# The rotation of a recurrence by columns instead of by pairs of heads

## What is computed

```python
w_log = -softplus(-(w0 + tanh(wd) @ w2)) - 0.5
decay = exp(-exp(w_log))
a = sigmoid(a0 + ad @ a2)
kk = k * k_k;  kk = kk / max(norm(kk), 1e-12)          # per head of 64
k = k * (1.0 + (a - 1.0) * k_a)
# 8 heads; the scan runs over 1024 tokens, computed in chunks of 64
state, y = scan(rwkv7_step, state0, (r, decay, k, v, -kk, kk * a))
y = groupnorm(y) * lnx_g + lnx_b
bonus = sum(r * k * r_k, axis=-1) * v
y = y + bonus
# beside it: attention of 8 heads over a band of 576 keys, on other columns of the same projection
x = x + gate * (concat([y_r * silu(g_r), y_a * silu(g_a)]) @ w_out)
```

## Time and profile before

| | us |
|---|---|
| median of 3 runs (2422.2 to 2427.26) | 2424.62 |
| the profiled execution's own time | 2418.48 |
| its span in the trace | 2416.6 |
| mean granted TensorE clock of it, share of full speed | 0.972 |

### The profile page before, as it was taken

The page is one execution under the profiler, slowest core; times in us unless marked ns, Lnnn a source line. Parts: engine busy times, 40 slices in busy tenths (PEclk is TensorE's granted clock), DMA queues, the critical chain, the costliest instruction groups (busy, mean ns, idle before and its releaser), DMA issues. The chain is left out here.

```text
span 2416.6 us, 43216 instructions
## 1 busy us (share of the span) xinstructions
PE 2277.8 (94%) x18830; PEld 1848.8 (77%) x18830; DVE 1456.7 (60%) x2456; ACT 937.6 (39%) x1532; POOL 78.7 (3%) x61
## 2 busy tenths in 40 slices
PE   7999988999999999999999999999999998789789
PEld 5777767788888888888878888778777776567667
DVE  5575866565434886777753454646455655767743
ACT  4446432444333443333342433354333232335441
POOL 0000000000000000000000000002000001200000
PEclk9999989999999999999999999989999999799989
DMA  5332252544123232222365534333323113111044
GB/s 179 88 94 66 69 170 71 173 123 129 53 62 119 77 96 83 79 79 86 93 196 164 157 90 135 98 113 110 109 80 107 51 37 97 41 44 44 3 129 150
DMA packets 329349, 238.15 MB, mean 99 GB/s; under 512 B 10948, under 2 KB 288580, under 8 KB 329032
## 3 DMA queue, kind: packets, MB, share of 16 engines
q1 hardware_dynamic: 326424, 229.82, 31.7%
q10 hardware_dynamic: 2736, 5.57, 0.6%
HBM read 202.33 MB, written 33.03 MB: 97 GB/s over the span
## 5 line engine op out<-in xcount | busy, mean ns | idle before, releaser
L1525 PE MATMUL PS<-SR 128*128 128x512 f32 (+2 forms) x1696 | 681.6, 402 | 43.2 <-DVE SR L2106 34.8
L1526 PE MATMUL PS<-SR 128*128 128x512 f32 (+2 forms) x1696 | 659.9, 389 | 0.0
L1527 PE MATMUL PS<-SR 128*128 128x512 f32 (+2 forms) x1696 | 659.7, 389 | 0.0
L2106 DVE TENSOR_TENSOR SR<-SB,SR 128x1024 fp32r<-128x1024 f32 (+1 forms) x240 | 289.1, 1206 | 289.8 <-ACT SR L2967 289.5
L1525 PEld LDWEIGHTS PS<-SR 128*128 128x128 f32 (+1 forms) x1696 | 320.4, 189 | 128.3 <-DVE SR L2106 36.9
L1527 PEld LDWEIGHTS PS<-SR 128*128 128x128 f32 (+1 forms) x1696 | 320.2, 189 | 68.7
L1526 PEld LDWEIGHTS PS<-SR 128*128 128x128 f32 (+1 forms) x1696 | 320.9, 189 | 62.2 <-issue 1.7
L2967 ACT ACTIVATE SR<-SB 128x1024 fp32r<-128x1024 f32 (+1 forms) x240 | 247.5, 1033 | 254.9 <-DMA SB<-in_w_down 116.1
L1546 PE MATMUL PS<-SR 128*128 128x512 f32 x624 | 243.4, 390 | 0.3 <-DVE SR L2232 0.3
L1548 PE MATMUL PS<-SR 128*128 128x512 f32 x624 | 242.8, 389 | 0.0
L1547 PE MATMUL PS<-SR 128*128 128x512 f32 x624 | 242.7, 389 | 0.0
(11 more groups left out here) (315 smaller groups left out, 3032.2 us busy)
## 6 DMA issues: line engine op xcount, KB each, us to landing
SB<-in_w_in SPq DMA_DIRECT2D x110, 512.0 KB, 4.0
SB<-in_w_up SPq DMA_DIRECT2D x88, 256.0 KB, 3.3
SB<-in_w_out SPq DMA_DIRECT2D x32, 512.0 KB, 4.2
SB<-in_w_down SPq DMA_DIRECT2D x32, 512.0 KB, 4.1
SB<-in_w_ada SPq DMA_DIRECT2D x12, 1024.0 KB, 5.2
hidden<-SB SPq DMA_DIRECT2D x22, 512.0 KB, 3.4
SB<-hidden SPq DMA_DIRECT2D x43, 256.0 KB, 5.3
asides<-SB SPq DMA_DIRECT2D x36, 256.0 KB, 4.1
```

The costliest lines, as they stand in the source:

```text
L1525: pe.matmul(out, whi[:, k - k0, :], hi[k], start=(k == 0), stop=False)
L1526: pe.matmul(out, whi[:, k - k0, :], lo[k], start=False, stop=False)
L1527: i = pe.matmul(out, wlo[:, k - k0, :], hi[k], start=False, stop=(k == j.K - 1))
L2106: v.tensor_tensor(m.f32r(a, kn * cn), m.f32(a, kn * cn), m.f32r(a + 1024, kn * cn).bitcast(F32), SUB).then_inc(*on("split.v", p))
```

## The change

A turn of the rotation now takes one recurrence step's 128 columns of all four tiles (`prep_a(half, c)`, `c` 0 to 3) instead of one tile's 512 columns. `pres` starts step `cp` as soon as its own turn (`("rot", cp)`) has been written, and turns 1 1 to 1 3 stand between recurrence steps 4 and 5. The key norm `kn` and the scratch A, B, C, D get places of their own in memory (one set in place of up to three), taken from 4096 words per partition that the build had reserved and the kernel did not use (`dynamic_dma_scratch_size=SCRATCH`, `TOTAL` larger by 4304); the table of ones and zeros for the scan moves to another place and is loaded earlier (`load_resets`). 1 + (a - 1) k_a is made by four ACT instructions on 128 columns each; the scan is four scans of 128 columns; the bonus's factor r_k goes into the small matrix that PE multiplies by (`rkbo`). The bonus is copied out once per turn.

```diff
-        self.kn, self.rot = part(26624, work(8192, 2048)), part(28672, work(10240, 2048))
+        self.kn = [tiles(v3(work(32816, 2048), 4)) for _ in range(2)]
+        self.rot = [work(34864 + 512 * i, 512) for i in range(4)]
...
     def prepare(self, half, places):
-        yield from self.room((places, 1))
-        b, free = places.take()
-        ahead = half
-        for j in range(4 + ahead):
-            if j < 4:
-                yield from self.after(("lora", half, j), *["v1"] * (half and j % 2))
-                yield [("prep_a", half, j)]
-            if j >= ahead:
-                yield [("prep_m", half, j - ahead, b, free), ("prep_b", half, j - ahead)]
-        places.give(b, ("prep.v", "bon", half))
-        yield [("prep_bon", half, b)]
+        yield from self.after(("lora", half, 3))
+        for c in range(4):
+            if half and c > 1:
+                yield from self.after(("read", 2 + c))
+            yield [("prep_a", half, c)]
+            yield from self.room((places, 1))
+            b, free = places.take()
+            places.give(b, ("prep.v", "bon", half, c))
+            yield [("prep_m", half, c, b, free), ("prep_b", half, c), ("prep_bon", half, c, b)]
+            self.done.add(("rot", 4 * half + c))
...
     def pres(self):
-        yield from self.after("prep0", "gemm0")
+        yield from self.after("gemm0")
         for cp in range(8):
-            if cp > 1:
-                yield from self.after(("seq", cp - 2))
-            if cp == 4:
-                yield from self.after("prep1", "g1")
+            yield from self.after(("rot", cp), f"g{cp // 4}", f"v{cp // 4}", *[("seq", cp - 2)] * (cp > 1))
             yield from self.pre(cp)
...
     def prepared(cp):
-        half = cp // 4
-        w.wait_ge(*at("prep.v", "9", half, 3))
-        w.wait_ge(*at("prep.g", "c", half, 3))
+        w.wait_ge(*at("prep.v", "9", cp // 4, cp % 4))
+        w.wait_ge(*at("prep.g", "c", cp // 4, cp % 4))
...
+    def prep_a(half, c):
+        A, B, C, D = m.rot
+        sl = slice(128 * c, 128 * c + 128)
+        w.wait_ge(*at("prep.a", "1", half, c))
+        w.wait_ge(*at("hs.v", "o", f"kk{half}", 3))
+        v.tensor_tensor(m.kk4[:, :, sl], h4(A), m.kk4[:, :, sl], MUL).then_inc(*on("prep.v", "1", half, c))
         w.wait_ge(*at("rs64", 0))
+        w.wait_ge(*at("lora.a", "s", half, 0, 3))
+        for e in turn_before(half, c):
+            w.wait_ge(*e)
+        for j in range(4):
+            i = v.tensor_tensor_scan(B[:, 128 * j:128 * j + 128], m.rs64[:, 0:128], m.sg[half][j][:, sl], 0.0, MUL, ADD)
+        i.then_inc(*on("prep.v", "4", half, c))
+        w.wait_ge(*at("prep.v", "4", half, c))
+        v.tensor_tensor(h4(A), h4(B), m.sg4[half][:, :, sl], SUB).then_inc(*on("prep.v", "5", half, c))
+        w.wait_ge(*at("shift.v", "o", f"r{half}", 3))
+        v.tensor_tensor(h4(D), m.rr4[half][:, :, sl], m.kk4[:, :, sl], MUL).then_inc(*on("prep.v", "3", half, c))
...
+    def prep_a(half, c):
+        A, B, C, D = m.rot
+        w.wait_ge(*at("lora.a", "s", half, 1, 3))
+        w.wait_ge(*at("shift.v", "ka"))
+        if half + c:
+            n = 4 * half + c - 1
+            w.wait_ge(*at("prep.v", "9", n // 4, n % 4))
+            w.wait_ge(*at("prep.g", "c", n // 4, n % 4))
+        for j in range(4):
+            i = a.activation(A[:, 128 * j:128 * j + 128], m.aa[half][j][:, 128 * c:128 * c + 128], ACT.Identity, bias=m.kac[:, j:j + 1],
+                             scale=m.col("ka", j))
+        i.then_inc(*on("prep.a", "1", half, c))
+        w.wait_ge(*at("prep.v", "4", half, c))
+        a.activation(C, B, ACT.Exp, scale=EH).then_inc(*on("prep.a", "6", half, c))
```

More of the change, by code:

```diff
@@ L341, in second @@
         self.staging = [f32(X0 + 512 * i, 512) for i in range(8)]
-        self.lw, self.rs64 = (f32(X0 + 4096 + 512 * i, 512) for i in range(2))
+        self.lw = f32(X0 + 4096, 512)
+        self.rs64 = self.fixed["cst"][:, CST["mst"][0]:CST["mst"][0] + 512]
         self.hrr = self.f32r(X0 + 5120, 512)
@@ L1393, in rotated @@
         else:
-            yield from self.after(("seq", 2), "k1", "qk1")
+            yield from self.after("k1", "qk1")
         yield (yield from self.head_norm(f"kk{half}", self.eight))
@@ L1397, in rotated, with widened @@
         yield from self.prepare(half, self.eight)
-        self.done.add(f"prep{half}")
-        if half:
-            for i in range(2):
-                self.P.give(3 + i, ("hs.pe", "o", "kk1", 3), ("lora.pe", 1, 3), ("prep.v", "9", 1, 3))
-                self.PT.give(2 + i, ("hs.pe", "o", "kk1", 3), ("prep.v", "9", 1, 3), ("prep.g", "c", 1, 3), ("prep.pe", 1, 3))
+    def widened(self):
+        yield from self.after("kk1", ("lora", 1, 3), "v1", "open")
+        for i in range(2):
+            self.P.give(3 + i, ("hs.pe", "o", "kk1", 3), ("lora.pe", 1, 3))
+            self.PT.give(2 + i, ("lora.pe", 1, 3), ("shift.v", "o", "v1", 3), ("hs.pe", "o", "kk1", 3))
     def lora_of(self, half):
@@ L1476, in compose @@
         self.mark("ml")
-        self.emit(("x_again",), *[("mix_part", 0, k) for k in range(8)])
+        self.emit(("x_again",), ("load_resets",), *[("mix_part", 0, k) for k in range(8)])
         self.P, self.PT = Places([]), Places([])
@@ L1500, in compose @@
                   chain(self.last_norms(0), self.flagged("spill0", ("spill", 0))), self.rotated(0), self.lora_of(0), chain(self.after("kk0"), self.norms_qk(0)),
-                  self.seqs(), self.pres(), self.outs(), self.rotated(1), self.lora_of(1), self.norms_qk(1),
-                  *[self.lane(units) for _ in range(3)], self.ended())
+                  self.seqs(), self.pres(), self.outs(), self.rotated(1), self.lora_of(1), chain(self.after("qk0"), self.norms_qk(1)),
+                  *[self.lane(units) for _ in range(3)], self.widened(), self.ended())
         self.emit(("end",))
@@ L2769, in prep_bon @@
+    def prep_bon(half, c, b):
+        w.wait_ge(*at("prep.pe", half, c))
         for par in range(2):
@@ L3539, in consts @@
         spilled()
[L3540 removed]
+        for name, to, what in (("lw", m.lw, "lora"), ("m2", m.m2, "m2")):
             sp.dma_start(to, d[what]).then_inc(*on(name, 0, by=16))
```

148 lines of the change are left out of this document (60 added, 88 removed), and 2 rows, old and new, of the table wide.

## The result

The changed kernel takes 2432.02 us (median of 6 runs, 2431.28 to 2436.76), the kernel before on the same chip 2423.16 (2421.38 to 2427.26): ratio 1.0042, 95% interval 1.003 to 1.0053. It is slower by 8.9 us; the forecast was 2420, faster. The profiled execution of the changed kernel took 2436.76 us, the longest of its six, and the one before is 4.7 us under its median; so the two traces lie further apart than the medians.

The account below looks back on a forecast made before the run. After the projections, a chain alternating between PE and DVE with in-order queues was taken as the bound. Terms -25 + 17 - 4 + 6 + 1.3 = -4.7 gave 2413.8 us; with the median 6.1 above the profiled execution, 2420 (2407 to 2432).

Parts of the forecast that it names:

- Start of step 4: After the last projection: `pre_ar` of step 4 can start near 2059 instead of 2084.4, 25 us earlier (22 to 27).
- Returned between `pre_ar` 4 and `seq_mean` 7: Steps 4 to 7: turns now inside the chain cost 19.7 us, 4.2 absorbed, plus 1.5 for PE: +17 (12 to 26).
- Tail of step 7: From `seq_mean` 7 to `seq_out` 7: one band instead of three stands ahead of `seq_out`, -4 us (0 to -6).
- Behind the end: Around `fin0`, where PE is nearly full: band work moves there, +6 us (3 to 7).
- Before the wall: Where r1 is written: the recurrence is one level further behind, PE waits 1.3 us of it, +1.3 (0 to 3).
- Rival 2: Steps 4 to 7: turns cost full price and POOL's work hits the chain; slower, near 2431 us; chance 0.22.
- Rival 1: Start of step 4 and the chain: the earlier start is mostly given back; 2420 us (2412 to 2425); chance 0.42.
- Rival 4: Behind the projections: PE's idle time only moves, nothing measurable changes, +5 at worst; 2423 to 2428 us; chance 0.16.
- Rival 3: Chain and tail: more is kept, return only 12 and tail 6; sum -14, near 2410 us; chance 0.20.

Follow-up runs that it names:

- Second profile: The changed kernel measured again, unedited, for another trace and more rounds: 2433.05 us, ratio 1.0049 to the kernel before.
- The first experiment: Changed kernel with all four turns of half 1 written ahead of step 4, each in its new form: 2428.69 us, ratio 1.0035.
- The fifth experiment: The second experiment's kernel with ACT's 1 + (a - 1) k_a and POOL's first product written right behind the turn before, in half 1: 2418.03 us, ratio 0.9992.
- The ninth: The eighth's kernel with turn 1 3 no longer held back to step 5, so turns 1 2 and 1 3 both stand in step 4: 2417.69 us, 0.9987.
- the eighth: The fifth experiment's kernel with turn 1 0 beside the last projection, planned in single tiles, and step 4 starting behind turn 1 0: 2408.36 us, ratio 0.9945.
- the second experiment: Changed kernel with only the planner's costs of a turn altered, so recurrence step 2 stands four steps ahead of r1's last tile: 2424.16 us, ratio 1.0011.
- the sixth: Changed kernel with other planner's costs, putting level 0 of recurrence step 2 23 steps ahead of r1's last tile: 2423.38 us, ratio 1.0009.
- the twelfth: The second experiment's kernel with filler products of the identity, read by nothing, where PE waits behind the wall: 2429.76 us, ratio 1.0033.

## Why the prediction was wrong

The mechanism was the one forecast, and the sum lost its sign to two terms that were too small. Second profile of the changed kernel against the earlier trace rows:

- *Start of step 4*, forecast -25 (22 to 27): -22.0. The size is at the edge of its bounds, the path is another. DVE is through with turn 1 1's first half at 2066.75, and `pre_ar` 4 waits on for PE, and PE for ACT: the copies of `pre_x`'s results (L3327) stand behind that turn's three exponentials.

```profile
2067.25 1.06 ACT L3327 ACTIVATE SB<-PS 128x512 f32<-128x512 f32 x2
2068.46 1.98 PE L1936 MATMUL PS<-SB 64*64 64x64 f32 x64 [2.97 <-ACT SB L3327]
2070.50 1.29 DVE L2806 TENSOR_TENSOR SB<-PS,SB 128x512 f32<-128x512 f32 x2 [3.74 <-PE PS L1936]
```

Two sizes were off as well: ACT's four pieces take 1.65 us (0.26 each was a read from PSUM), and the scans of turn 1 0 2.43 beside POOL, of which my bound was 1.7.

- *Returned between `pre_ar` 4 and `seq_mean` 7*, forecast +17 (12 to 26): +23.4, and +27.4 in the first profile (the bound of 26 is 25.3 by its own terms). **This is the first step that failed**: I let 27% of the turns' DVE time, 4.2 us, fall into idle time, off a full price of 19.7 us with the waits for ACT. The first experiment puts the same turns outside the chain, with as many bands finished in the stretch, and the stretch is 23.9 us shorter: on balance nothing was absorbed, and the full price was too low. Steps 4 and 5 grew by 29.6 us, steps 6 and 7 fell by 6.2, with two more bands in the former and one less in the latter. Ahead of `pre_t0` the four operations of `prep_a` cost 4.3 us a turn where I had 4.4: the scans took 1.07 more beside POOL, and the difference, which I had at 1.6, took 0.69. What was too small is DVE's wait for ACT, 2.6 and 4.6 us in place of 2 and 2, and POOL's hold on what I had priced at nothing: 1.1 in `pre_t0` of step 4, 1.6 in a band's product and 0.9 in a copy of step 5. With the 4.2 us not absorbed these add to 11, more than the 6.4 by which the term missed (10.4 in the first profile), so part of them is given back; which part was not taken apart. The fifth experiment agrees: operations ahead, 3.7 less and step 5 11.8 less. The ninth against the eighth shows that the same turns in another order cost 9.0 more, with two more bands in the stretch.
- *Tail of step 7*, forecast -4 (0 to -6): -2.3.
- *Behind the end*, forecast +6 (3 to 7): +7.3; the bands' own PE time is +6.0. Right.
- *Before the wall*, forecast +1.3 (0 to 3): +5.9 (4.4 in the first profile), and 8.9 in the time with the costs of the second experiment. **This is the second step that failed.** I priced one level's waits of PE. The level itself is 3.2 us, and with it came the wait of 2.76, the products of `seq_out` 1 and a stretch at the lower clock, 7.9 us together up to the end of step 2's levels; 7.4 are left at `pre_ar` 3 and 5.9 at the copies. That more lead than the second experiment's wins nothing clear is shown by the sixth. How the 7.9 divide between the pieces is worked out from the trace and not tested; the 1.5 us by which the 8.9 exceed the 7.4 of the copies lie behind `pre_ar` 4, in a stretch whose order is the same.

The terms of the second profile add to +12.4 before rounding; the medians of those runs differ by 12.0.

Rival 2, to which I gave 0.22, came true in kind: the stretch grew by more than 22, and its two reasons, full price and POOL, are there, with longer waits for ACT as a third that it lacks. Its time, 2431 against 2432, is partly luck: its sum of +5 to +7 had 1.3 ahead of the wall, where 4.4 to 5.9 were lost, and the measured differences are 8.9 and 12.0. The Trainium skill ("SBUF — State Buffer", section "SBUF: two separate sides") says that a GpSimd instruction holds the shared port for its whole length; the traces agree in kind, +1.07 us on the scans beside a POOL product of 1.77. Rival 1's own ground, PE's idle time, was a share of a stretch and not of the place where the turns stand. Rival 4's balance (+5 at worst) left out the wall. Rival 3 did not come.

PE's lower clock in step 4 (0.79 against 1.00) is a rival that the experiments bound and do not exclude. In the twelfth 1.8 us came back with the higher clock, which the filler had taken; behind `pre_kn` of that step the same clock brought nothing. In the eighth's order, where less of the filler was used, it came with a step 4 shorter by 3.8. Step 5 had 0.88 in the changed kernel and 0.90 before and grew more than step 4, so its mean clock does not explain it.

## What to carry to other kernels

Work moved from an empty stretch into a chain was paid here at its whole length from the step that it stood ahead of, with every wait of its own for another engine (23.9 us against a full price of 19.7); a share of idle time taken over the stretch was no discount. Look instead for a place beside a full engine: turn 1 0 beside the last projection took 10 us off the kernel that had all else the same (2418.03 to 2408.36). When a change touches a planner's costs, compare the order in places that the change does not name: three such numbers gave back 8.9 us of a loss of 12.0. And before filler is put on an engine to raise its clock, see whether the engine's next result is waited for: the filler's own time comes first.
